# Later loads of the convolution state on ScalarE's queue, and matmuls of constants in TensorE's waits before the experts

## What is computed

```python
proj = x @ w_in + b_in                       # q, k, v and the two convolution inputs ca, cg
attn = sliding window attention (128), rotary positions, a learned sink per head
u    = ca * sigmoid(cg)
u_ext = concatenate([conv_prefix, u])        # for the sample tokens the prefix is state_conv (30 rows)
conv = silu(layer_norm(causal depthwise conv, width 31, of u_ext))
h    = layer_norm(ALPHA * x + concatenate([attn, conv]) @ w_out + b_out)
# hier_moe: best of 4 groups, best two of its 8 experts; a token's two experts are SwiGLU, width 256
f    = sum over the two experts of gate * ((silu(h @ w1[e]) * (h @ w3[e])) @ w2[e])
y    = layer_norm(ALPHA * h + f)
```

## Time and profile before

| | |
|---|---|
| Median of 3 runs | 1473.01 us (1471.99 to 1474.28) |
| The profiled execution | 1474.07 us, its span 1472.2 us |
| TensorE matmul busy | 1309.1 us, 89% of the span |
| ScalarE busy | 593.0 us, 40% |
| VectorE busy | 583.5 us, 40% |
| GpSimd busy | 380.5 us, 26% |
| HBM | 202.04 MB read, 62.78 MB written |

### The profile page before, as it was taken

The page is one execution under the profiler, slowest core; times in us unless marked ns, Lnnn a source line. Parts: engine busy times, 40 slices in busy tenths (PEclk is TensorE's granted clock), DMA queues, the critical chain, the costliest instruction groups (busy, mean ns, idle before and its releaser), DMA issues.

```text
span 1472.2 us, 20676 instructions
## 1 busy us (share of the span) xinstructions
PE 1309.1 (89%) x5827; PEld 649.4 (44%) x5828; DVE 583.5 (40%) x1787; ACT 593.0 (40%) x883; POOL 380.5 (26%) x530
## 2 busy tenths in 40 slices
PE   7949999998999998899999994899999999999800
PEld 3314444666666655345555553333333333333300
DVE  1404343444555555466666555011111111111158
ACT  0000000242445433333333331466666666666445
POOL 5103120000000000355555552122323333333134
PEclk9969999999999999999999996899999999999955
DMA  9423334131122173345554321369899888998684
GB/s 381 155 62 106 114 99 146 54 105 55 54 71 73 58 229 121 113 173 172 180 184 153 119 103 58 119 185 338 225 327 319 279 264 273 344 342 282 192 289 191
DMA packets 83135, 261.55 MB, mean 178 GB/s; under 512 B 15384, under 2 KB 34080, under 8 KB 69894
## 3 DMA queue, kind: packets, MB, share of 16 engines
q1 hardware_dynamic: 62775, 216.26, 40.5%
q0 software_dynamic: 12320, 40.93, 11.8%
q10 hardware_dynamic: 7959, 3.43, 0.9%
HBM read 202.04 MB, written 62.78 MB: 180 GB/s over the span
## 4 chain that ended last, share of the span: by engine, by line
PE 56%; issue 27%; DMA 6%; DVE 3%; ACTq 3%; ACT 2%; POOL 1%; SPq 1%; POOLq 1%; DVEq 0%
PE P L996 11%; PE bank_S L1020 9%; PE P L843 7%; PE M L996 6%; PE bank_S L843 6%; PE bank_S L670 4%; PE P L670 2%; PE bank_T L978 2%; PE M L670 2%; PE bank_T L670 2%; PE M L861 2%; ACTq L1072 2%; DMA const<-in_consts 2%; DMA big<-in_w 1%; DMA work<-conv_rows 1%
## 5 line engine op out<-in xcount | busy, mean ns | idle before, releaser
L996 PE MATMUL P<-big,work 128*64 x416 | 186.9, 603 | 2.7 <-ACT work L1208 2.4
L997 PE MATMUL P<-big,work 128*64 128x512 f32 x416 | 187.1, 603 | 0.0
L709 PE MATMUL P<-big,work 128*128 128x256 f32 (+1 forms) x512 | 173.9, 496 | 0.0
L1236 ACT ACTIVATE big<-big 128x2048 f32 x78 | 144.8, 1903 | 29.4 <-issue 18.7
L1020 PE MATMUL bank_S<-big,work 128*64 x312 | 143.9, 604 | 3.7 <-ACT big L1242 3.1
L1022 PE MATMUL bank_S<-big,work 128*64 128x512 f32 x312 | 143.9, 604 | 0.0
L709 PEld LDWEIGHTS P<-big,work 128*128 128x128 f32 x512 | 97.4, 194 | 70.8 <-issue 64.2
L843 PE MATMUL P<-big,work 128*128 128x512 f32 x256 | 116.2, 608 | 2.7 <-DVE work L1474 2.7
L1689 DVE COPY work<-M 128x256 f32<-128x256 f32 x39 | 16.5, 424 | 253.8 <-PE M L1006 253.8
L843 PE MATMUL bank_S<-big,work 128*128 128x512 f32 x256 | 113.3, 595 | 0.0
L996 PEld LDWEIGHTS P<-big,work 128*64 128x64 f32 x416 | 55.5, 138 | 126.1 <-issue 126.1
(11 more groups left out here) (301 smaller groups left out, 2315.2 us busy)
## 6 DMA issues: line engine op xcount, KB each, us to landing
big<-in_w SPq DMA_DIRECT2D x96, 1024.0 KB, 9.0
work<-in_xt_prompt SPq DMA_DIRECT2D x32, 512.0 KB, 3.7
big<-in_toe SPq DMA_DIRECT2D x16, 512.0 KB, 3.5
work<-in_x_prompt SPq DMA_DIRECT2D x16, 512.0 KB, 4.0
h_rows<-work SPq DMA_DIRECT2D x16, 512.0 KB, 2.7
sum_rows<-work SPq DMA_DIRECT2D x16, 512.0 KB, 3.6
big<-sum_rows SPq DMA_DIRECT2D x16, 512.0 KB, 9.0
out_y_prompt<-big SPq DMA_DIRECT2D x16, 512.0 KB
```

The costliest lines, as they stand in the source:

```text
L709: last = mm(dst[0:n, 0:c1 - c0], lhs[:, k, :], w_qkv[:, k, c0:c1], start=(k == 0), stop=(k == KD - 1))
L996: mm(lower, xgT[:, k, 0:U], both[:, k], start=(k == 0), stop=(k == KD - 1))
L997: last = mm(upper, xgT[:, k, U:P], w_up[:, k], start=(k == 0), stop=(k == KD - 1))
L1236: fn(w_up.rearrange("p k m f -> p m k f")[:, :, ks, :], src, ACT.Copy).then_inc(s[f"wu{part}_ok"], 1)
```

## The change

ScalarE issues the two loads of the convolution state behind the sigmoid of tile 9 instead of tile 3; the key cache's load stays where it is. TensorE gets a helper `keep_awake(count)`, which runs `count` matmuls of two constants (the 128x128 identity and 512 columns of the rotary table) into PSUM bank P1. Nobody reads their result. It is called in six places: 4 before the router of step 17 (with a wait for VectorE's last read of P1 in the sweep), 3 before the rank of step 17, 6 before the rank of step 18, 6 before the wait for the table of blocks, 14 before the wait for `eids_ok`, and 2 between the first block's turn and its `up`.

```diff
+            def keep_awake(count):
+                for _ in range(count):
+                    mm(P1[:, :], ident, C["rope"][:, 0:512], start=True, stop=True)
...
                 if 0 <= c - 2:
                     if c == 2:
                         after(pe, s["at_ev"], NT - 1)
+                    if c == NT + 1:
+                        after(pe, s["o1_ev"], NT - 1)
+                        keep_awake(4)
                     router(c - 2)
                 if c <= NT:
                     project_out(c, 1, "pe_o1")
+                if c == NT + 2:
+                    keep_awake(6)
                 if 0 <= c - 2 and c - 1 != NT:
                     rank(c - 2)
                 if 0 <= c - 1 <= NT:
                     turn_h(c - 1)
                 if c - 1 == NT:
+                    keep_awake(3)
                     rank(c - 2)
 
+            keep_awake(6)
             pe.wait_ge(s["tab_build"], 1)
...
             last.then_inc(s["pe_tab"], 1)
+            keep_awake(14)
             pe.wait_ge(s["eids_ok"], 1)
...
             turn(0, 0, 0)
+            keep_awake(2)
             for b in range(RING):
                 up(b, b, 0)
...
                 if i == 3:
                     act.wait_ge(s["pair_sum"], 4)
                     act.dma_start(Ks[0:WIN - 1], a["cache_k"][:, 1:WIN, :].rearrange("b s n -> s b n")).then_inc(s["s_cache"], 16)
+                if i == 9:
                     for j in range(2):
                         src = a["state_conv"].rearrange("(i b) j n -> i (b j) n", i=2)[j]
                         act.dma_start(state_n[0:NROW, j], src).then_inc(s["s_cache"], 16)
```

## The result

| | before | after |
|---|---|---|
| Median | 1472.5 us (1471.08 to 1474.28, 4 runs) | 1449.12 us (1447.68 to 1453.88, 4 runs) |
| Ratio | | 0.9834, 95% interval 0.9811 to 0.9858 |
| Profiled execution, span | 1474.07, 1472.2 us | 1448.8, 1446.9 us |
| TensorE matmul busy | 1309.1 us, 5827 instructions | 1329.3 us, 5897 instructions |

A forecast was written before the change was run, and what follows sets the result against it. Bound: TensorE's matmuls, except a 25.93 us ScalarE DMA issue in the input stage; after the sweep, waits and a fallen clock. 1474.07 - 26.6 - 0.75 = 1446.7; from the median, 1473.0 - 27.35 = 1445.7 us, range 1443.0 to 1450.0.

The forecast's parts named there:

- Part 1: Input stage: state's loads behind tile 9 remove TensorE's idle 24.27 us and 2.1 us at low clock; taken as 26.6.
- The forecast's second way: Input stage: pair 1 to pair 2 takes 50.59 us, the undisturbed pair 24.03, so 26.56 us to gain.
- the tiles of pair 2: Input stage: tiles have 4.0 us to spare; 4.7 more beside the key cache's load would be 0.7 late; taken as nothing.
- C: Input stage: pair 2's tiles late by the key cache's transfer, 0.7 up to 3 us; time up to 1448.7; chance 0.06.
- D: Input stage: SyncE's issues held up while ScalarE's queue is being filled, 13.5 us lost; time 1459; chance 0.03.
- E: The 26 us belong to the state's own loads and come again at tile 9; time 1472.3, no change; chance 0.03.
- part (d): At tile 9: the state's two issues take 0.5 to 0.9 us, hidden by 2.2 us of cover before product 3.
- Part 2: Between output sweep and experts: 35 constant matmuls keep the clock up; first `up` ends 0.75 us earlier.
- A: The forecast itself: clock holds at full rate between sweep and experts; time 1445.7 us; chance 0.72.
- B: Between sweep and experts: clock falls all the same, first `up` ends 2.1 us later; time 1448.5; chance 0.11.
- sign of failure: Prediction fails if the stage from 88 to 863 doesn't simply move up by 26.6 us.

The follow-up runs named there:

- cache_spread: Kernel before, no constant matmuls, state's loads still behind tile 3, key cache's load cut into 112 and 15 partitions: 1445.79 us, ratio 0.98.
- second trace: Trace of the changed kernel run again unaltered: 1451.96 us (6 runs), ratio 0.9854 to the kernel before.
- 7 of 14: Changed kernel with 7 instead of 14 constant matmuls ahead of the wait for the first gathered rows: 1448.54 us, ratio 0.9815.
- third trace: Trace of the changed kernel run once more unaltered: 1449.57 us (5 runs), ratio 0.9827 to the kernel before.
- part 2 alone: Kernel before plus only the constant matmuls, state's loads still behind tile 3: 1474.48 us (12 runs), ratio 1.0017.
- Part 1 alone: Kernel before with only the state's loads moved behind tile 9, no constant matmuls: 1445.63 us, ratio 0.9816; once more 1446.31 us, ratio 0.9791.
- spread_fitted: Changed kernel with constant matmul groups fitted to their waits, key cache's load in two pieces, state's loads back behind tile 3: 1440.94 us, ratio 0.9772.
- fill_fitted: Changed kernel with constant matmul groups cut to 3, 3, 4, 4, 9, 1 and one more between rank 15 and router 16: 1443.81 us, ratio 0.9771.

## Why the prediction held, and where it missed

**Part 1** was right in its mechanism and nearly in its size. 24.27 us of idleness and 2.1 us at the low clock went; 25.3 to 25.5 us came between pair 1 and pair 3 in the five traces with part 1 in the table above, against the 26.6 forecast. The most that could come is 74.46 - 48.06 = 26.40, which cache_spread got. The forecast's second way gave 0.16 more because it set a start of the timeline (64.24) against one of the chain of waits (114.83, where the timeline has 114.67). The missing 0.9 to 1.1 is the step that I had weighed and put at nothing: the tiles of pair 2. I allowed them 4.7 us more on the way by the row of a store, subtracted 4.0 to spare, got 0.7 and took 0. They took 4.7 more (9.0 against 4.3 in the landing times) and TensorE lost 0.8 to 1.1. So C came, near the 0.7 us of its nearest row. That the two 4.7 agree to the digit is luck, but the reason was the right one: at 96 us, with nothing else of ScalarE's on the way, the one-engine load alone makes the same store take 7.0 us instead of 2.7. D, that SyncE's issues would be held too, is out: SyncE issued the tiles at 79.80, on time, and already in the kernel before it issued, while ScalarE was held from 68.45 on:

```profile
69.19 0.44 SPq L424 DMA_DIRECT2D big<-u_rows  x1
```

(The Trainium skill, Perfetto Trace Analysis, "DMA Instruction — HWDGE (DVE, Sync)", would have the generator locked for one sequencer; the traces don't show such a lock between SyncE and ScalarE, whose issues went on side by side for 0.44 us and 25.93.) E is out by 0.79 us of issue at tile 9, which part (d) put at 0.5 to 0.9.

The Trainium skill, DMA: Bandwidth & Descriptors, "Why a DMA increments its semaphore by 16 and not by 1", says that a slowest dimension of 127 goes to one DMA engine and that the number of engines is the largest divisor up to 16. The runs agree: 112 partitions landed 448 KB in 4.3 us, where 127 needed over 26.

**Part 2** missed by 1.7 us in the first trace: 0.75 us of gain forecast, 1.0 us of loss measured in the stage (57.78 to 58.74). The step that failed there is the assumption of A that the clock holds in the gaps. It was B that came, between 872 and 876: after three fillers and a rank, 0.64 us of idleness and a router of 36 columns, the clock fell while TensorE was never idle for more than 0.64 us, and the six fillers took 6.73 us (B had said some 7). It came in the second trace too and with 7 of 14, but not in the third trace nor in part 2 alone. There A came true almost to the digit: the first turn 2.8 us later relative to turn 15 (2.7 forecast), the end of the first `up` 0.7 us earlier (0.75). So A at 0.72 and B at 0.11 were wrong as chances: the same instructions meet the fall in three of five traces.

B's place was right and its price too high. Router(16) still ran mostly at full clock (2.32 us, not 3.6), so the end of the first `up` came 1.0 us late, not 2.1. The 2.1 was also added up wrongly: B's first turn at 929.6 plus the 9.7 us that A takes from there to the end of the first `up` gives 939.3, not 938.3, so +3.2, and a time of 1449.6. The fourteen took 12.1 us from start to start, as forecast, but began late, so the first turn started 4.4 us later relative to turn 15, not 2.7. With the two corrections, 1.1 us for C and up to 1.7 for B, the forecast would have been 1446.8 to 1448.5.

**The range** of 1443.0 to 1450.0 held the median by 0.9 us, and that was partly luck. It was made from the spread of three runs, 1.3 us; the later runs show a spread of single executions of 1444.57 to 1455.46 for the same kernel, and one of this kernel's two later medians, 1451.96, lies outside. In the profiled execution 4.3 us won between pair 3 and turn 15 made up for 1.1 lost at pair 2, 1.0 before the experts and 2.6 in their stage. The prediction had named it a sign of failure if the stage from 88 to 863 didn't simply move up; it didn't, but that stage differs by as much between traces of one kernel. (The chances of A to D add up to 0.92, not 0.94.)

**Open.** Part 1 alone is 3.8 us (0.9 to 6.7) faster than the changed kernel. The edited stage doesn't show it: its mean is 57.9 us in the four traces with the full filling and 57.4 in the six without fillers. The experts' stage shows about 2 (444.4 to 444.8, and 447.3 for part 2 alone, against 441.9 to 443.2 for before and part 1 alone). The stage's weight loads end some of its waits. But cache_spread, without constant matmuls, has 444.31, and with them spread_fitted has 441.14 and fill_fitted 445.52. I can't say whether the constant matmuls lengthen that stage, nor where the 3.8 us are. Why the clock falls in some executions and not in others also stays open.

## What to carry to other kernels

The DMA issues that took long here were waiting for the transfer in front of them in their queue. Where you meet one, look at how many engines that transfer runs on (its DMA share, 0.07 here) and cut its leading dimension into a multiple of 16 and a rest, rather than move what stands behind. In these runs matmuls of constants won only where each group ended with its wait or before: sum each group's time against the wait it stands in, since past that every one costs its 0.86 us on the path. And when a run takes away a suspected cause and the effect stays, look first at what stands in its place at that moment: the store at 70 us stayed late, the one at 96 didn't.

## What the runs showed of the hardware

- A load of 127 partitions and 508 KB (rows of 512 bytes) ran at 0.07 of 16 engines, held the next issue of its queue for 26 us right behind it and for 14 us when that came 23 us later; issues of the other queue went on in 0.3 to 0.4 us each meanwhile. The reverse order held nothing.
- In both cases the held issue was let go when some 900 of the load's 1016 packets had gone (902 and 901).
- It also made transfers of another queue late that were spread over all engines: 9.0 us to landing instead of 4.3 for two loads of 512 KB, 7.0 instead of 2.7 for a store of 256 KB.
- The granted clock fell to 1.2 GHz in a stretch in which TensorE was idle for 0.64 us at most but ran narrow matmuls (36 and 32 columns) and turns. It did so in three of five traces with the same instructions there; in the three traces with one more full-width matmul between rank and router, and shorter groups around it, it held.
- Single executions of one kernel scatter by 10 to 15 us here. In the traces the attention and sweep stage differs by 6 us (with how long the clock is low in it) and the last layer norm by 5, with no order by kernel.
